# A streaming encoder layer in one launch: first loads reordered, gate spill in groups of sixteen, one-hots scaled by ScalarE alone

## The reference, cut to what matters

```python
def layer(x, mk, mv, ...):
    x = x + token_mixer(rmsnorm(x, ln_mix_w), ...)       # w_in, gated conv, SSD scan, w_out
    x = x + cross_attn(rmsnorm(x, ln_mem_w), mk, mv, ...)  # w_mq, softmax over 256 rows, w_mo
    x = x + peer(rmsnorm(x, ln_ffn_w), w_pq, sub_keys, u_tab, v_tab)

# peer, for each token and each of 8 heads:
    v1, i1 = lax.top_k(sc[:, :, 0], 16)
    v2, i2 = lax.top_k(sc[:, :, 1], 16)
    comb, cidx = v1 + v2 (all 256 pairs), i1 * 128 + i2
    top_sc, pos = lax.top_k(comb, 16)
    eidx = take_along_axis(cidx, pos)
    gate = softmax(top_sc)
    hid  = gelu(xb . u_tab[eidx])            # 128 experts of 16384 per token
    out  = sum_k gate * hid * v_tab[eidx]
```

## Time and profile before

| | |
|---|---|
| median of 3 runs | 1850.4 us (1849.38 to 1851.29) |
| the profiled execution | 1853.36 us, its span 1851.3 us |
| busy, share of the span | PE 91%, PE weight load 68%, DVE 66%, POOL 37%, ACT 20% |
| DMA | 563 MB, mean 304 GB/s |
| gathers (queue q0) | 302 MB, 42.3% of 16 engines' span |
| loads and stores by SP (q1) | 243 MB, 35.9% |
| gate spill by ACT (q10) | 33,024 packets, 16.78 MB, 3.0% |

### The profile page before, as it was taken

How to read it: one execution, slowest core, us unless ns; L and a number is a source line. 1 busy time by engine, 2 the same in 40 slices (tenths; PEclk the granted TensorE clock), 3 DMA queues, 4 the chain that set the end, 5 groups by cost and what they waited for, 6 DMA issues and landing times. The chain is left out here.

```text
span 1851.3 us, 19837 instructions
## 1 busy us (share of the span) xinstructions
PE 1690.1 (91%) x7088; PEld 1256.2 (68%) x7088; DVE 1224.9 (66%) x2437; ACT 372.9 (20%) x914; POOL 693.5 (37%) x598
## 2 busy tenths in 40 slices
PE   6998999989747998899887999999999999999996
PEld 5887888877635676687776566666666666666542
DVE  1262211699687868798986899776656666656675
ACT  2032123111321244551661001101000000000101
POOL 0000000134123438640755455555444544444551
PEclk9999999999877998899989899999999999999998
DMA  5532443679244968994999999999999999999995
GB/s 167 173 114 91 159 137 127 232 244 363 81 154 154 363 222 303 353 364 138 331 356 414 410 408 410 409 408 409 410 410 410 402 409 410 397 410 403 381 402 228
DMA packets 238300, 563.09 MB, mean 304 GB/s; under 512 B 17068, under 2 KB 125276, under 8 KB 236156
## 3 DMA queue, kind: packets, MB, share of 16 engines
q0 software_dynamic: 82944, 302.03, 42.3%
q1 hardware_dynamic: 122236, 243.04, 35.9%
q10 hardware_dynamic: 33024, 16.78, 3.0%
HBM read 539.46 MB, written 21.66 MB: 303 GB/s over the span
## 5 line engine op out<-in xcount | busy, mean ns | idle before, releaser
L770 POOL DMA_INDIRECT M<-in_u_tab,IDX x288 | 324.8, 1128 | 743.5 <-DVE PEER L1717 361.0
L777 POOL DMA_INDIRECT M<-in_v_tab,IDX x288 | 365.1, 1268 | 383.2 <-DVE X L1738 308.3
L1079 PE MATMUL PSB<-XN,M 128*128 128x256 f32 x2048 | 468.6, 384 | 9.8 <-ACT M L1289 4.5
L1087 PE MATMUL PSB<-M,HST 128*128 128x512 f32 x1024 | 460.8, 596 | 12.0 <-DVE HST L1800 10.7
L1079 PEld LDWEIGHTS PSB<-XN,M 128*128 128x128 f32 x2048 | 393.5, 193 | 109.9 <-issue 52.6
L1717 DVE CUSTOM_DVE_ANT_0 M<-M,XN 128x1024 f32<-128x1024 f32 x288 | 351.5, 1222 | 144.4 <-DMA M<-in_u_tab,IDX 125.1
L1738 DVE SCALAR_TENSOR_TENSOR X<-M,PEER,X 128x1024 f32<-128x1024 f32 x256 | 327.8, 1281 | 107.3 <-DMA M<-in_v_tab,IDX 94.0
L819 PE MATMUL PSB<-M 128*128 128x256 f32 (+1 forms) x1408 | 334.1, 399 | 10.7 <-DVE M L1376 9.4
L1087 PEld LDWEIGHTS PSB<-M,HST 128*128 128x128 f32 x1024 | 195.0, 191 | 216.2 <-issue 200.4
L819 PEld LDWEIGHTS PSB<-M 128*128 128x128 f32 x1408 | 271.4, 194 | 67.1 <-DVE M L1376 10.3
L826 PE MATMUL PSB<-M 128*128 128x256 f32 (+1 forms) x1056 | 250.3, 398 | 6.0 <-DVE X L1591 5.4
(11 more groups left out here) (213 smaller groups left out, 1038.4 us busy)
## 6 DMA issues: line engine op xcount, KB each, us to landing
M<-in_u_blocks SPq DMA_DIRECT2D x128, 512.0 KB
M<-in_v_tab SPq DMA_DIRECT2D x128, 512.0 KB
M<-in_w_in SPq DMA_DIRECT2D x24, 1024.0 KB
M<-in_w_pq SPq DMA_DIRECT2D x16, 1024.0 KB
gate_spill<-M ACTq DMA_DIRECT2D x16, 1024.0 KB
M<-gate_spill SPq DMA_DIRECT2D x16, 1024.0 KB
M<-in_w_out SPq DMA_DIRECT2D x8, 1024.0 KB
M<-in_w_mq SPq DMA_DIRECT2D x8, 1024.0 KB
```

The source lines that it names most:

```text
L770: pool.indirect_dma_start(out=UA[:, s % RR, :], out_offset=None, in_=utab, in_offset=bass.IndirectOffsetOnAxis(ap=IDX[:, n:n + 1], axis=0) ...
L777: pool.indirect_dma_start(out=VA[:, s % RR, :], out_offset=None, in_=vtab, in_offset=bass.IndirectOffsetOnAxis(ap=IDX[:, n:n + 1], axis=0) ...
L1079: last = pe.matmul(PSB[:, 4 + b % 2, 0:2 * P], UBLK[:, b % SR, c, :], XN[:, 1:3, c * P:(c + 1) * P], start=(c == 0), stop=(c == DC - 1))
L1087: last = pe.matmul(PSB[:, 2 * t + hf, :], WR[:, b % WRING, t * P:(t + 1) * P], VBLK[:, b % SR, hf * 512:(hf + 1) * 512], start=(b == 0), s ...
```

## The change

1. `GRP` 8 becomes 16 and `GRING` 3 becomes 2: the gates go out in 1 KB pieces instead of 512 B, and come back in eight groups of 2 MB, two of them buffered, instead of sixteen of 1 MB, three buffered. The two buffers lie elsewhere in SBUF.
2. x tile 1 is loaded ahead of the small vectors. The transposes and copy of the SSD state are a job of their own (`state`) behind the first four `in` jobs. ACT runs a square root of a constant first, which loads its table early.
3. For dense tile 1 DVE compares only the second keys (128x512 elements). ACT makes the scaled half from `iota` alone: |key - iota|, then relu(gate - gate * that), four instructions of each. DVE makes -gate once (`BACK`). The plan counts 0.7 us for DVE's part instead of 1.25.

```diff
-GRP = 8
-GRING = 3
+GRP = 16
+GRING = 2
@@ dense
-            s += [("memn", "gc v".split().index(b))]
+            s += [("state",)] * (b == "gc") + [("memn", "gc v".split().index(b))]
@@ dve_us
+    if x[:2] == ("oh", DENSE[0]):
+        return 0.7
@@ buffers
-        GR = [ar(off, NCH, GRP, CH_TOK) for off in (12488, 6656, 8704)]
+        GR = [ar(off, NCH, GRP, CH_TOK) for off in (6144, 10240)]
+        BACK = TT[:, 1, 2, :]
@@ sync
             load_block(sp, 0)
+            sp.dma_start(X[:, 1, :], xp[1]).then_inc(x_in[1], 16)
...
             sp.dma_start(S0[:, :, :], a["state_ssd"]...).then_inc(state_in, 16)
-            sp.dma_start(X[:, 1, :], xp[1]).then_inc(x_in[1], 16)
@@ tensor
+            def state():
                 pe.wait_ge(state_in, 16)
                 transposes("hi", [S0[:, x, :] for x in range(4)])
...
                 pe.wait_ge(oh_done, m + 1)
+                pe.wait_ge(hot_done, m + 1)
@@ scalar, oh
-                act.wait_ge(hot_done, m + 1)
-                for j in range(OH_TOK):
-                    first = hot_buffer(t, n)[:, j, 0, :]
-                    last = act.activation(first, first, ACT.Copy, scale=TT[:, d, 2, c + j:c + j + 1])
+                hot = hot_buffer(t, n)
+                if d == 0:
+                    if n == 0:
+                        wait_drained(act, ("tt", 1))
+                    if n >= OH_RING[0]:
+                        wait_job(act, ("gb", t, n - OH_RING[0]))
+                    for j in range(OH_TOK):
+                        away = act.activation(hot[:, j, 0, :], iota[:, :], ACT.Abs, bias=TT[:, 0, 0, c + j:c + j + 1], scale=-1.0)
+                    link(away)
+                    for j in range(OH_TOK):
+                        last = act.activation(hot[:, j, 0, :], hot[:, j, 0, :], ACT.Relu, bias=TT[:, 0, 2, c + j:c + j + 1],
+                                              scale=BACK[:, c + j:c + j + 1])
+                else:
...
             act.wait_ge(const_ok, 1)
+            act.activation(PSM[:, 0:1], EPSC[:, :], ACT.Sqrt)
@@ vector, tt and oh
                 if t == 1:
                     b = begin(("tt", 1))
+                    link(dve.tensor_scalar(BACK, b[:, 2 * P:3 * P], -1.0, None, ALU.mult))
                 else:
                     dve.wait_ge(tt_done, 1)
+                    dve.wait_ge(oh_done, P // OH_TOK)
...
+                if d == 0:
+                    part = [P, OH_TOK, P]
+                    dve.tensor_tensor(hot[:, :, 1, :], bc(iota[:, :].unsqueeze(1), part), bc(TT[:, 0, 1, c:c + OH_TOK].unsqueeze(2), part),
+                                      ALU.is_equal).then_inc(hot_done, 1)
+                    return
```

More of the change, by code:

```diff
@@ L290, in jobs_of @@
     if k == "const":
-        return [("sm", "D"), ("hi", "D")]
+        return [("sm", "D")]
+    if k == "state":
+        return [("hi", "D")]
     if k == "turn":
@@ L1096, in fold @@
                 last.then_inc(fold_done, 1)
-            does = {"const": const, "turn": turn, "memn": memn, "in": in_, "dt": dt, "z": z, "oc": oc, "kv": kv, "kt": kt,
+            does = {"const": const, "state": state, "turn": turn, "memn": memn, "in": in_, "dt": dt, "z": z, "oc": oc, "kv": kv, "kt": kt,
                     "s1": s1, "s2": s2, "s3": s3, "s4": s4, "ho": ho, "o": o_, "q": q_, "a1": a1, "a2p": a2p, "a2": a2, "mo": mo,
@@ L1293, in oh @@
                 m, c = d * P // OH_TOK + n, n * OH_TOK
-                act.wait_ge(hot_done, m + 1)
-                for j in range(OH_TOK):
-                    first = hot_buffer(t, n)[:, j, 0, :]
-                    last = act.activation(first, first, ACT.Copy, scale=TT[:, d, 2, c + j:c + j + 1])
+                hot = hot_buffer(t, n)
[11 more added lines that the diff above has]
+                else:
+                    act.wait_ge(hot_done, m + 1)
+                    for j in range(OH_TOK):
+                        last = act.activation(hot[:, j, 0, :], hot[:, j, 0, :], ACT.Copy, scale=TT[:, 1, 2, c + j:c + j + 1])
                 last.then_inc(oh_done, 1)
@@ L1814, in final @@
                 dve.scalar_tensor_tensor(out=x, in0=x, scalar=rs, in1=GAIN[0:n, :], op0=ALU.mult, op1=ALU.mult).then_inc(y_norm, 1)
-            does = {"const": const, "norm": norm, "turn": turn, "memn": memn, "in": in_, "keep": keep, "ca": ca, "cs": cs, "dt": dt, "oc": oc,
+            does = {"const": const, "state": state, "norm": norm, "turn": turn, "memn": memn, "in": in_, "keep": keep, "ca": ca, "cs": cs, "dt": dt, "oc": oc,
                     "kt": kt, "s1": s1, "s2": s2, "s3": s3, "s4": s4, "o": residual("o"), "a1": a1, "mo": residual("mo"),
```

## The result

The changed kernel takes 1870.1 us in the median of 4 runs (1868.3 to 1878.6), against 1850.9 for the kernel before, run beside it. The ratio is 1.0101, with a 95% interval of 1.0079 to 1.0122: slower by about 1%. I had forecast slower, but by 4.7 us.

A forecast was written before the change was run, and what follows sets the result against it. PE and the DMA engines were taken as both full from about 1020 us, so edits count by that stage's start. +0.5 + 7.2 - 3 = +4.7 us on the profiled 1853.4 gives 1858.1, or 1855 for the median; range 1843 to 1866.

The forecast's parts named there:

- The start: Kernel start: later small vectors, an earlier first norm and the moved state transposes together cost -0.0 to +1.1, taken as +0.5 us.
- The cost of the state's transposes: At the start, behind the fourth `in` job: the four transposes delay ACT's norm of the memory, +0.6 to +1.1 us.
- Tile 1's gates: Some 690 to 825 us: ACT's one-hots set the pace and PE work moves behind the gates, net +7.2 us.
- Sum 119.3, so the last `gb` ends near 810, 15.5 us earlier: Tile 1's gates from 690.8: 14 pairs at 7.7 us (107.8), +7.0 for the norm's pair and 4.5 allowed.
- my allowance of 4.5: Tile 1's gates: 4.5 us for gelus with their table loads and attention copies on ACT, worked out from no row.
- 22.7 us of PE work moved behind the gates: After tile 1's last `gb`: the plan moved five `pq` and one set of `sc` there, 22.7 us with no gap to fill.
- The clock rival: Tile 1's gates: PE's clock falls with ACT's gaps, about nine pairs losing 1 us each, +9, so 1864; chance 0.12.
- ACT keeps up: Faster rival: ACT's pair in tile 1's gates at or under 7.1 us, gates -1 to -4, last stage -6; 1843; chance 0.25.
- My estimate of the pace by its figure, 7.8: Tile 1's gates: with the skill's 93 ns per pointer operand, the relus' step would be 0.39 and the pace 7.8 us.
- Into the last stage: Just before the last stage: `vd` start taken as 0, earlier u blocks shorten PE's stall and slow clock, -3 us (-9 to +4).
- an edit pays (or costs) by the moment at which this stage starts: Last stage, from about 1020 us: PE and DMA both full, so only its start counts; first `vd` moves -2.9 to +3.6 us.
- the -1 that I gave "by the page": Into the last stage: if 512 B pieces already reach line rate, the spill gains nothing and this part is -1 instead of -3.

The follow-up runs named there:

- only_loads: The kernel before with only the reordered first loads, the state's own job and the early square root; ratio 0.9993 (0.9975 to 1.0010).
- price_alone: The kernel before with only the plan's price of tile 1's one-hots set to 0.7 us instead of 1.25, VectorE still making them; ratio 1.0138.
- change_price_16: The changed kernel with the plan's price of tile 1's one-hots at 1.6 us instead of 0.7; ratio 1.0006 against the kernel before.
- price_20: The kernel before with only the plan's price of tile 1's one-hots set to 2.0 us instead of 1.25; ratio 0.9967.
- extra_bytes: The kernel before with eight more 0.5 MB copies into scratch DRAM, one behind every tenth vd from 20 to 90; ratio 1.0050.

## Why the prediction was wrong

**The start** (+0.5 forecast): -2.5 in the profiled pair, but only_loads shows no effect, and traces of equal code vary by 9 us. Of the details the first was as worked out: PE's first work moved from 9.50 to 10.82 us, the first transposes of x from 12.99 to 12.60, here as timeline rows of the changed kernel:

```profile
10.82 0.42 PE L817 MATMUL PSB<-ident,EARLY 112*128 112x112 f32 x1 [10.82 <-DMA EARLY<-in_cache_conv_ssd]
12.60 1.97 PE L817 MATMUL PSB<-ident,XN 128*128 128x128 f32 x8 [1.36 <-DVE XN L1417]
```

The cost of the state's transposes (+0.6 to +1.1) didn't come: they took 0.60 us, PE's wait for the memory's norm was 2.62 us instead of 2.89, and the transposes behind it began at 37.67 instead of 39.17.

**Tile 1's gates** (+7.2 forecast, +15.7 measured). The step that failed is "Sum 119.3, so the last `gb` ends near 810, 15.5 us earlier". From the second pair's end (690.2) to 816.4 it took 126.2 us. The sizes of the activations were right (1.59 us for four relus forecast, 1.65 measured; 5.7 us for two `oh`, 5.72 measured). The pace was not 7.7: the eight pairs from 705.43 to 769.22 took 7.97 each, where 7.84 is the mean of a pair with and without a spill and the rest is mostly a gelu with its table load; that is 3.8 us over 14 pairs. The pair with the norm took 19.5 us (769.22 to 788.71) and not 14.7, since ScalarE starts the norm only behind two sets of one-hots and PE idles 5.63 us; my allowance of 4.5 was somewhat too large. Another 1.9 us came before the second pair's end, a stretch that I had put at no change (from `tt 1` 42.6 us, before 40.7). In all the last `gb` came 6.7 us sooner after `tt 1`, not 15.5. The other half of the step, 22.7 us of PE work moved behind the gates, was right: 62.9 - 40.5 = 22.4. And -6.7 + 22.4 is the 15.7.

But the larger fault is in what I took for the cause. I set the moved 22.7 us against a faster end of the gates, as if the closer plan brought it, and let only ScalarE's pace decide how much faster. price_alone shows that the plan's number does the harm with ScalarE's work untouched, at no earlier end of the gates at all (175.3 us behind `tt 1`, before 175.5), and change_price_16 that most of the loss goes away with the number. A hint was at hand: with DMA at 1.05 and VectorE waiting for gathers, packing closer promises little. I used that bound only against a pace below 6.9 us, and didn't ask what the plan alone would do.

The clock rival did not come: the granted clock of stretch A is 0.95 after against 0.94 before. "ACT keeps up" fell with the 1.65 us and the pace of 7.56, above its 7.1. VectorE's compare was put at 0.6 us and took 0.69, which changes nothing, since it waits for PE.

By the Trainium skill (ScalarE: Activation LUTs, What ACT_TABLE_LOAD costs) a pointer operand adds about 93 ns; the trace agrees, 479 - 387 = 92 for the second. My estimate of the pace by its figure, 7.8, was the better one.

**Into the last stage** (-3 forecast, +1.9 measured). The direction of each detail came: SP's wait went, the u block stall went, the gates stood before the gathers. But their size was off: the first `vd` moved by 10.7 us, where I had at most 3.6 in all and 6.5 for these loads. What failed is "an edit pays (or costs) by the moment at which this stage starts", the first `vd`. In the 17 traced kernels without extra bytes that moment lies 150.6 to 163.9 us behind the dense work, and stretch B is 969 to 978 us long, with the late ones hardly longer: 968.8 and 969.9 us with a first `vd` at 151, 970.7 and 970.0 at 162. Stretch B is a load of some 381 MB (384 in price_20, which does a few gathers fewer before it) at 390 to 394 GB/s. So the stalls that I counted as gains were slack that the transfers filled, and the moment that counts is, to within a few us, the end of the dense work. extra_bytes shows it from the other side. (The -1 that I gave "by the page" doesn't follow either: no term of the -3 was the spill's.)

**The spill's packets:** in the stretch 691 to 700 us 1040 packets of 1 KB with a share of 33.1% are 46 ns each, inside the 41 to 56 given.

```profile
q10 hardware_dynamic: 1040, 1.05, 33.1%
```

Against twice 28 ns that is 10 ns less for 1 KB, some 5 us of all sixteen engines over the eight spills of tile 2. Stretch B is no shorter for it: 970.0 and 970.7 us with the larger pieces, 968.8 and 969.9 without. The Trainium skill (DMA: Bandwidth & Descriptors, Specifications) has pieces of 512 B reach line rate already: the time agrees, the single packet (18 B/ns at 512 B, 22 at 1 KB) doesn't.

## What to carry to other kernels

When a stage is full of transfers, find the last moment before it from which the bytes are a fixed load, and value every edit by that moment; to shorten waits inside the full stage paid next to nothing here. A cost in a planner's table is an edit of its own, and has to be run apart from the code whose cost it states: here VectorE's instruction did fall from 1.20 to 0.69 us, and telling the planner so made the kernel slower than it is with a price of 1.6, since the gates were held by gathers in one kernel and by ScalarE in the other. Work that waits for something else was best spread over all the products that could cover it, which a price above its own duration brought about.

## What the runs showed of the hardware

A second per-partition operand costs ScalarE somewhat more than the first: 309, 387 and 479 ns for none, one and two on 128x128 elements (medians; the three are different functions). A gate between 0 and 1 can be put into a one-hot with Relu(gate - |difference|), with a number as scale, at 390 ns.

TensorE idled 20.74 us beside full DMA engines, and the first `vd` came 10.7 us later after the dense work than before; that was free to within 2 us. PE's busy share in the stage behind gave no hint of it: it stands at 20.00 of 20 us, with the DMA engines full as well, and 4.2 MB more still cost 10.4 us there, not where the copies ran but where late gathers held ScalarE and ScalarE held PE.
